# Third block's head outputs by token rows, and a router with early logits and roots by token, in a two-layer hybrid decoder step

## The reference

```python
def _mixer_c(h, hg_s, lower_bound, w_in, hg_gn, w_out):        # 8 heads of 128
    qp, fp, ip, gp = split(h @ w_in)
    f = lower_bound + (1 - lower_bound) * sigmoid(fp)
    q, k, v = silu(qp), 1 - f, ip
    o, s_new = _hgrn2(q, k, log(f), v, hg_s)                   # gated linear recurrence with carried state
    o = o * rsqrt(mean(o**2, over a head's 128) + EPS) * hg_gn * silu(gp)
    return o @ w_out, s_new

def _moe(h, w_router, b_router, wg, wu, wd):                   # h = rmsnorm(x)
    logits = h @ w_router + b_router
    top_val, top_idx = top_k(logits, 2)
    gates = scatter(softmax(top_val), top_idx)
    return sum over e of gates[:, e] * swiglu(h, wg[e], wu[e], wd[e])
```

## Time and profile before

| | |
|---|---|
| runs | 1507.21, 1500.73, 1492.23 us |
| the profiled execution: its time | 1492.97 us |
| its span | 1491.1 us |
| mean granted clock of TensorE | 0.996 |
| third block with its output projection, from its first tile to the router | about 481 to 704 us |
| router, up to the first expert product | 704.5 to 726.4 us |
| one expert round | 93.47 us |
| HBM over the span | 270 GB/s; in the rounds 382 GB/s |

### The profile page before, as it was taken

How to read it: one execution, slowest core, us unless ns; L and a number is a source line. 1 busy time by engine, 2 the same in 40 slices (tenths; PEclk the granted TensorE clock), 3 DMA queues, 4 the chain that set the end, 5 groups by cost and what they waited for, 6 DMA issues and landing times.

```text
span 1491.1 us, 22842 instructions
## 1 busy us (share of the span) xinstructions
PE 1468.7 (98%) x8429; PEld 1303.5 (87%) x8429; DVE 1123.0 (75%) x1228; ACT 912.2 (61%) x953; POOL 86.4 (6%) x96
## 2 busy tenths in 40 slices
PE   9999999999999999999999999999999999999997
PEld 8899899999999999998888888888888888888885
DVE  5766688455456577456798888988889898898987
ACT  5434655433333553343777878778787787877875
POOL 1024110000000001210200000000000000000011
PEclk9999999999999999999999999999999999999999
DMA  9477725996446443442999999999999999999994
GB/s 253 129 129 143 152 89 142 303 302 186 134 141 184 150 140 103 138 141 66 414 383 393 388 361 396 374 388 390 359 394 377 386 392 359 393 378 385 398 333 171
DMA packets 213586, 404.02 MB, mean 271 GB/s; under 512 B 13471, under 2 KB 130491, under 8 KB 213390
## 3 DMA queue, kind: packets, MB, share of 16 engines
q1 hardware_dynamic: 202976, 372.82, 71.9%
q0 software_dynamic: 6320, 22.20, 5.0%
q10 hardware_dynamic: 4222, 8.06, 1.4%
HBM read 372.75 MB, written 30.28 MB: 270 GB/s over the span
## 4 chain that ended last, share of the span: by engine, by line
PE 92%; DVE 5%; ACT 1%; issue 1%; POOL 0%; ACTq 0%; DVEq 0%; POOLq 0%
PE bank L525 27%; PE bank L527 27%; PE bank L526 27%; PE bank L754 2%; PE bank L1190 1%; PE bank L1014 1%; DVE dense_lo L1924 1%; PE bank L799 1%; PE bank L699 1%; DVE arena L2074 1%; PE bank L746 1%; PE bank L1127 1%; PE bank L675 0%; PE bank L1117 0%; PE bank L707 0%
## 5 line engine op out<-in xcount | busy, mean ns | idle before, releaser
L2414 DVE TENSOR_TENSOR w_lo<-arena,w_hi 128x2048 fp32r<-128x2048 f32 (+1 forms) x280 | 597.0, 2166 | 82.9 <-ACT w_hi L1761 82.0
L1761 ACT ACTIVATE w_hi<-arena 128x2048 fp32r<-128x2048 f32 (+1 forms) x280 | 502.1, 1820 | 117.4 <-PE bank L527 111.8
L525 PE MATMUL bank<-w_hi,xg_hi 128*128 128x512 f32 x704 | 275.6, 391 | 0.7 <-DVE w_lo L2414 0.5
L527 PE MATMUL bank<-w_hi,xg_lo 128*128 128x512 f32 x704 | 274.1, 389 | 0.0
L526 PE MATMUL bank<-w_lo,xg_hi 128*128 128x512 f32 x704 | 274.0, 389 | 0.0
L1924 DVE TENSOR_TENSOR dense_lo<-ring,dense_hi 128x2048 fp32r<-128x2048 f32 (+1 forms) x77 | 165.5, 2149 | 120.6 <-ACT dense_hi L1415 120.5
L1415 ACT ACTIVATE dense_hi<-ring 128x2048 fp32r<-128x2048 f32 (+1 forms) x78 | 140.5, 1802 | 133.1 <-PE bank L527 113.0
L525 PEld LDWEIGHTS bank<-w_hi,xg_hi 128*128 128x128 f32 x704 | 132.2, 188 | 31.0 <-issue 3.1
L527 PEld LDWEIGHTS bank<-w_hi,xg_lo 128*128 128x128 f32 x704 | 132.1, 188 | 27.7
L526 PEld LDWEIGHTS bank<-w_lo,xg_hi 128*128 128x128 f32 x704 | 132.2, 188 | 26.9
L525 PE MATMUL bank<-h_hi,dense_hi 128*128 128x320 f32 x448 | 141.9, 317 | 1.4 <-DVE h_lo_a L1994 1.1
(11 more groups left out here) (448 smaller groups left out, 2312.7 us busy)
## 6 DMA issues: line engine op xcount, KB each, us to landing
arena<-in_w_moe_down SPq DMA_DIRECT2D x176, 512.0 KB, 6.7
arena<-in_w_moe_gate SPq DMA_DIRECT2D x128, 512.0 KB, 7.3
arena<-in_w_moe_up SPq DMA_DIRECT2D x128, 512.0 KB, 7.4
arena<-in_w_moe_gate SPq DMA_DIRECT2D x64, 384.0 KB, 4.2
arena<-in_w_moe_up SPq DMA_DIRECT2D x64, 384.0 KB, 5.3
ring<-in_w_in_ab SPq DMA_DIRECT2D x32, 512.0 KB, 8.6
ring<-in_w_in_c SPq DMA_DIRECT2D x32, 512.0 KB, 4.8
expert_rows<-ZERO SPq DMA_DIRECT2D x12, 1024.0 KB, 7.8
```

The costliest lines, as they stand in the source:

```text
L525: mm(out, left[0], right[0], start=start, stop=False)
L527: return mm(out, left[1], right[0], start=False, stop=stop)
L1761: fn(WH[SLOT_OF[p]][:, 0:unit_size(p)], STAGE[:, s, 0:unit_size(p)], ACT.Copy).then_inc(S("unit_hi"), 1)
L2414: v.tensor_tensor(WL[w][:, 0:n], STAGE[:, s, 0:n], WH[w][:, 0:n].bitcast(F32), ALU.subtract).then_inc(S("unit_split"), 1)
```

## The change

Output rows. `out` puts the probabilities (128x128) and, per sample, a matrix of queries on the stationary side, and the values or the states (128 columns) on the moving side, so that the result has tokens on the partitions. The query matrix of sample s is 128x64, zero but for that sample's 8 columns: a buffer `QB` for two heads, zeroed once by POOL at the first turn, its diagonal blocks copied by ScalarE (`spread_queries`). ScalarE copies the rows to `ROWS_OF` and squares them with its accumulator, which gives the sums per token (`SSH`). Root and reciprocal are of 128x18 and 128x6 numbers; VectorE scales the rows; three transposes per head (`rows_back`) bring them back, and VectorE's gate reads the transposed bank. `sq` and `varc` go; `gate` comes behind `mixc`, and the second `rootc` stands ahead of the last head's `state`.

Router. Logits of tiles 0 to 5 are multiplied ahead of the last output tile, 6 and 7 behind it. Mean squares are taken with the tokens on the partitions, as three columns; root and reciprocal are of 128x3 numbers; logits are scaled and biased after the transposes. The rank products are fp32r instead of float32. The first weight unit's low part comes after the ranks. The first block's loops are exchanged.

```diff
-    v1 ub0 mb0 lb0 v2 wh ub1 mb1 lb1 wl turn0 v3 ub2 mb2 lb2 out0 v4 sq0 ub3 mb3 lb3 state0 turn1 v5 wh ub4 mb4 lb4 wl out1 v6 sq1 ub5 mb5 lb5 state1 turn2 v7 ub6 lb6
-    out2 v8 wh sq2 ub7 lb7 state2 turn3 wl v9 lb8 kend1 part1 out3 v10 sq3 state3 v11 wh turn4 wl g0 out4 g1 wh sq4 wl state4
-    turn5 g2 out5 g3 wh sq5 wl state5 silug0 varc0 rootc0 turn6 g4 gate0 gate1 out6 g5 wh sq6 wl gate2 gate3 state6
-    turn7 mixc0 mixc1 g6 mixc2 mixc3 out7 h0 h1 g7 h2 h3 sq7 silug1 silug2 gate4 gate5 state7 gate6 gate7 wh mixc4 mixc5 wl
-    h4 h5 varc1 rootc1 mixc6 mixc7 h6 h7
+    v1 ub0 mb0 lb0 v2 wh ub1 mb1 lb1 wl turn0 v3 ub2 mb2 lb2 out0 v4 ub3 mb3 lb3 state0 turn1 v5 wh ub4 mb4 lb4 wl out1 v6 ub5 mb5 lb5 state1 turn2 v7 ub6 lb6
+    out2 v8 wh ub7 lb7 state2 turn3 wl v9 lb8 kend1 part1 out3 v10 state3 v11 wh turn4 wl g0 out4 g1 wh wl state4
+    turn5 g2 out5 g3 wh wl state5 silug0 rootc0 turn6 g4 out6 g5 wh wl state6 turn7 mixc0 gate0 mixc1 gate1 g6 mixc2
+    gate2 mixc3 gate3 out7 h0 h1 g7 h2 h3 silug1 silug2 rootc1 state7 mixc4 gate4 mixc5 gate5 wh wl h4 h5 mixc6 gate6
+    mixc7 gate7 h6 h7
...
+        ROWS_OF = [PH[:, u, 0:3 * P].rearrange("p (i n) -> p i n", n=P) for u in range(HG)]
+        QB = region(6400, 2, NB, SMP)
...
-                    mm(b[:, 0:NT], C("inv_d"), SQF[tag][:, 0, :], start=True, stop=False)
                     pe.wait_ge(S("n3_squares"), KD)
-                    ins = mm(b[:, 0:NT], C("inv_d"), SQF[tag][:, KD - 1, :], start=False, stop=True)
+                    for i, (t0, tn) in enumerate(BLK):
+                        mm(b[0:tn, i:i + 1], SQF[tag][:, 0, t0:t0 + tn], C("inv_d")[:, 0:1], start=True,
+                           stop=False).then_inc(S("unit_used"), 1)
+                        ins = mm(b[0:tn, i:i + 1], SQF[tag][:, KD - 1, t0:t0 + tn], C("inv_d")[:, 0:1], start=False, stop=True)
+                        if i < 2:
+                            ins.then_inc(S("unit_used"), 1)
...
+            def rows_back(u):
+                pe.wait_ge(S("rows_scaled"), u + 1)
+                kind = "dve" if u in HEADS[0] else "act"
+                b = open_bank(kind)
+                for i, (t0, tn) in enumerate(BLK):
+                    ins = nc.tensor.transpose(b[:, t0:t0 + tn], ROWS_OF[u][0:tn, i, :], ident[0:tn, 0:tn])
+                close_bank(kind, ins, ("hn1", "scale", u))
...
+            def output_rows(u):
...
+                pe.wait_ge(S("queries_spread"), u + 1)
+                b = open_bank("act")
+                mm(b[:, 0:P], p[:, 0:P], values(0), start=True, stop=True)
+                mm(b[:, P:TP], p[:, P:TP], values(0), start=True, stop=False)
+                mm(b[:, P:TP], p[:, TP:384], values(1), start=False, stop=True)
+                mm(b[0:SMP, TP:384], p[:, 384:448], values(2), start=True, stop=False)
+                for s in range(NB):
+                    ins = mm(b[0:SMP, TP:384], QB[:, u % 2, s, :], ST[:, u % NST, s, :], start=False, stop=(s == NB - 1))
+                close_bank("act", ins, ("num", 1, u))
...
                     if kind == "oc" and n == len(HEADS[0]) - 1:
                         for u in HEADS[1]:
-                            head_scale(heads, u)
+                            rows_back(u)
...
+                    if kind == "oc" and k == KD - 1:
+                        pe.wait_ge(S("router_in"), 32)
+                        early = open_bank("dve", 1)
+                        logits(range(KD - 2), early)
                     gemm_tile(w, k % 2 * P, src, "dve", (kind, k), KD)
...
+            logits([KD - 2], b).then_inc(S("unit_used"), 1)
+            close_bank("dve", logits([KD - 1], b), "logit_rows")
+            mean_squares("n3")
+            after_empty(pe, "logit_rows")
...
-                    mm(b[0:tn, i * NE:(i + 1) * NE], ones[:, 0:tn], SELM[:, j, :], start=(j == 0), stop=False)
+                    mm(b[0:tn, i * NE:(i + 1) * NE], everyone[:, 0:tn], CHOSEN[:, j, :], start=(j == 0), stop=False)
...
+            def spread_queries(u):
+                if u == 0:
+                    act.wait_ge(S("queries_zero"), 2)
+                if u >= 2:
+                    after_fill(act, ("num", 1, u - 2))
...
+                fn(own, Q[:, u, TP:NT].rearrange("p (s t) -> p s t", t=TS), ACT.Copy).then_inc(S("queries_spread"), 1)
...
                 elif name == "out":
-                    free(fn(OH[:, u, :], take(("num", 1, u))[:, 0:NT], ACT.Copy))
-                elif name == "sq":
-                    after_empty(act, ("num", 1, u))
-                    fn(SQH["hn1"][u], OH[:, u, :], ACT.Square).then_inc(S("hn1_squares"), 1)
+                    b = take(("num", 1, u))
+                    fn(ROWS_OF[u][:, 0:2, :], b[:, 0:TP].rearrange("p (i n) -> p i n", n=P), ACT.Copy)
+                    fn(ROWS_OF[u][0:SMP, 2, :], b[0:SMP, TP:384], ACT.Copy)
+                    spent = (Q[:, u, 0:P], Q[:, u, P:TP], K[:, u, 0:P])
+                    for i, (t0, tn) in enumerate(BLK):
+                        ins = fn(spent[i][0:tn], b[0:tn, i * P:(i + 1) * P], ACT.Square, accum_out=SSH[0:tn, u, i:i + 1])
+                    free(ins)
...
             split_high(0, 0, 0)
...
+            act.wait_ge(S("n3_scale"), 1)
...
                 elif name == "rootc":
-                    head_reciprocals("hn1", u)
-                elif name == "mixc":
-                    dve.wait_ge(S("gated1"), u + 1)
-                    scaled_head(OH, "hn1", u)
+                    at = slice(HEADS[u][0], HEADS[u][-1] + 1)
+                    dve.wait_ge(S("hn1_roots"), u + 1)
+                    step(v.reciprocal(SSH[:, at, :], SSH[:, at, :]))
+                    for h in HEADS[u]:
+                        v.tensor_tensor(ROWS_OF[h], ROWS_OF[h], SSH[:, h, :].unsqueeze(2).to_broadcast([P, 3, P]),
+                                        ALU.mult).then_inc(S("rows_scaled"), 1)
...
-            split_low(1, 0)
-            dve.wait_ge(S("unit_split"), 1)
+            step(v.memset(RANK[:, :, :], 0.0))
             b = take("ranks")
...
+            split_low(1, 0)
+            tokens_low(0, 0, 2)
             split_low(2, 1)
-            tokens_low(0, 0, 2)
+            tokens_low(0, 1, 2)
             split_low(3, 2)
-            tokens_low(0, 1, 2)
...
                 if name == "turn":
+                    if u == 0:
+                        pool.wait_ge(S("level_up1"), 2)
+                        pool.wait_ge(S("queries_zero"), 1)
+                        g.memset(QB[:, :, :, :], 0.0).then_inc(S("queries_zero"), 1)
+                        pool.wait_ge(S("queries_zero"), 2)
                     if u % 2 == 0:
                         after_empty(pool, (("V", 1, u // 4), u % 4 // 2, 2))
                     spread(1, u)
```

More of the change, by code:

```diff
@@ L244, in trunk_kernel @@
         HEADS = ((0, 1, 2, 3, 4, 5), (6, 7))
-        SQH = {"hn0": [region(NT * u, NT) for u in range(KD)],
-               "hn1": [region(5120 + NT * u, NT) for u in range(KD)]}
+        SQH = {"hn0": [region(NT * u, NT) for u in range(KD)]}
         ROT = region(13824, H4, NT)
@@ L325, in trunk_kernel @@
         NS0 = small[:, 24:56]
+        SSH = small[:, 432:432 + 3 * HG].rearrange("p (h i) -> p h i", i=3)
         NRAW = small[:, 56:92].rearrange("p (h n) -> p h n", n=9)
@@ L330, in trunk_kernel @@
         LBT = small[:, 144:168].rearrange("p (a b) -> p a b", b=8)
+        brt = small[:, 424:424 + NE]
         QE = small[:, 168:296].rearrange("p (a b) -> p a b", b=SMP)
@@ L357, in trunk_kernel @@
         CM2 = region(7384, 3, 64)
-        SELM = rows[:, 1, 0:3 * NE].rearrange("p (i e) -> p i e", e=NE)
+        BEATEN = rows[:, 1, 0:3 * NE].rearrange("p (i e) -> p i e", e=NE)
+        AT_COUNT = AT_ARENA + 26880 + (CONST["level"][0] + 128) // 32 * 32
+        COUNT, CHOSEN = parts("count_tiles", AT_COUNT, 2, P), parts("chosen_of", AT_COUNT + 2 * P, 3, NE)
+        SELM = CHOSEN[:, :, :].bitcast(F32)
         RANK = rows[:, 2, 0:3 * NE].rearrange("p (i e) -> p i e", e=NE)
@@ L896, in _ @@
                 elif name == "weigh":
[L897 removed]
+                    piece_along(outputs(u, PB[:, u % 2, :], lambda: after_empty(pe, ("sc", 0, u)), QE[:, u % 2, :]))
                 elif name == "state":
@@ L921, in n_rows, with logits @@
                 close_bank("act", ins, "n_out")
+            def logits(ks, b):
+                for k in ks:
+                    pe.wait_ge(S("n3_value"), k + 1)
+                    ins = mm(b[0:NE, 0:NT], wrt[:, k, :], U_R[:, k, :], start=(k == 0), stop=(k == KD - 1))
+                return ins
             def projection_out(kind, src, heads):
@@ L1061, in _ @@
                     pe.wait_ge(S("vx1"), 1)
-                    piece_along(outputs(1, u, PH[:, u, :], lambda: pe.wait_ge(S("chunks_parted"), u // 4 + 1), Q[:, u, TP:NT]))
+                    output_rows(u)
                 elif name == "state":
@@ L1753, in _ @@
             projected_out("oc", "n3")
-            root("n3")
+            b = take(("n3", "ms"))
```

(20 more changed lines are left out.)

100 lines of the change are left out of this document (41 added, 59 removed).

## The result

The changed kernel takes 1502.17 us, the median of 13 runs between 1497.99 and 1509.28. The kernel before, run beside it on the same chip, takes 1493.03 (13 runs, 1491.78 to 1507.21). The ratio is 1.0057, 95% interval 1.0040 to 1.0074: slower by 0.57%, where -1.0 us was forecast. The range of 1488 to 1508 holds 1502.17, but for a poor reason: it was built around 1500.73, the median of three runs, and the middle of thirteen is 7.7 us lower. Read as a difference, the forecast missed by 10 us. That 1502.17 lies close to the 1502.6 of my second rival, the falling clock, is luck of the same kind: the rival's difference was +1.3 to +2.4, the measured one is +9.1.

What follows compares the result with a forecast made beforehand. TensorE, busy 98% of the span, was taken to bound the kernel. Terms 0, -2.9, -1.3, +1.0, +3.4, -2.2 and +1.0 summed to -1.0 us: 1492.0 profiled, 1499.7 on the median, range 1488 to 1508.

Steps and rivals of the forecast that it cites:

- second rival, the falling clock: TensorE's clock falls to half at the block's end, ahead of the projection: sum +1.3 to +2.4 us, chance 0.2.
- Term 7: First turn: POOL's zeroing of the spread queries delays the spread and head 0's outputs: +1.0 us, bounds 0 and +2.1.
- Term 1: Output products of eight heads: 24 records at 0.11 take 2.6 us per head, as before: 0.
- Term 2: Variances of heads 0 to 5: twelve products go, 3.36 us, against a 0.5 stall before head 6's outputs: net -2.9.
- Term 3: Heads 0 to 3: three transposes (0.24 us) replace each scale (0.56): -1.3 us.
- Term 4: End of the block, heads 4 to 7: longer waits outweigh TensorE's savings: +1.0 us, bounds -2.4 and +2.0.
- Term 5: Router: six logits ahead of the last tile delay it and the first expert weight transfer: +3.4 us.
- Term 6: Router, from the last tile's end to the first block of expert inputs: -2.2 us, bounds -3.5 and 0.

Runs made afterwards that it cites:

- filled waits: The changed kernel with unused identity products on TensorE ahead of its waits for the first spread and the projection's first bank; 1497.82 us, ratio 1.0019.
- late spread: The kernel before, with POOL also waiting for VectorE's second level and zeroing 1024 columns ahead of its first spread; 1500.6 us, ratio 1.0046.
- late logits: The changed kernel with all eight logits behind the last output tile; 1498.4 us, ratio 1.0034.
- root behind states: The changed kernel with the second root behind the last head's new states in every engine's order; 1500.76 us, ratio 1.0045.
- spread first: The changed kernel with POOL's first spread ahead of the zeroing of the query buffer; 1496.55 us, ratio 1.0011.
- root ahead: Changed kernel with POOL's first spread ahead of the zeroing, all logits behind the last output tile, second root behind the last head's outputs; 1493.62 us, ratio 0.9997.
- low parts first: As root ahead, with the weight split's high part earlier, its low part later, and the transposes of heads 6 and 7 later; 1489.12 us, ratio 0.9976.
- its repetition: The same kernel as low parts first, run once more; 1490.15 us, ratio 0.9971.

## Why the prediction was wrong

- **Term 7, the zeroing ahead of the spread** (+1.0, bounds 0 to +2.1) is the step that failed. I took from the one case in the earlier trace rows that a spread begun inside a split ends 0.9 after that split. The mechanism was right; what I ended with the split goes on over every VectorE instruction with two SBUF operands that follows without a gap. 567.66 + 2.27, then 0.47, then four in 1.68: the spread got no turn between any two of them. The wait was 3.0 instead of 1.0, beyond my upper bound, and with the half clock that came with it A was 6.0 longer. The Trainium skill ("SBUF — State Buffer", section "Who interferes with whom") has the rule of which instructions contend and says that the loser waits in full; on the waiting the trace agrees (4.95), and it shows besides that the wait doesn't end with the first of VectorE's instructions. On an instruction that only writes it says little: the zeroing took 0.96, but only its last 0.15 lay beside the split. I had counted only the one winner that I knew from the trace of before, and not the run of them in VectorE's own timeline, which stood there to be read.
- **The rival "the clock falls"** was right as a mechanism and too small in place: I put it at the end of the block alone, and with 0.2. It came at the first head's outputs as well, where my own term 7 had put a standing (2.7 us), ahead of the projection (1.2) and through the router (E 13.23 against 11.63 with the full clock up to 721, 1.6). That is 5.5 us, against 8.7 in all; the first block, which before had 5.4 us of half clock in it and now has 3.6, gives 0.8 back. I had waits of TensorE in terms 4 and 7 of my sum, each at its bare length.
- **Term 1, output products** (0) measured +0.29 a head: from TensorE's timeline of the second head, given below, 588.90 to 591.77 is 2.87, where before it was 582.19 to 584.77, 2.58. The four value products take 1.03 where three took 0.82, and the states 1.84 where they took 1.76. Some +2.3 over eight heads, 2.0 of it in B.

```profile
588.90 0.39 PE L796 MATMUL bank<-arena 128*128 128x128 f32 x2
589.12 0.39 PE L797 MATMUL bank<-arena 128*128 128x128 f32 x2
589.35 0.39 PE L798 MATMUL bank<-arena 128*128 128x128 f32 x2
589.66 0.43 PE L799 MATMUL bank<-arena 128*64 128x128 f32 x2
589.93 1.91 PE L801 MATMUL bank<-arena 128*64 128x128 f32 x16
591.77 0.38 PE L530 MATMUL bank<-dense_hi,h_hi 128*128 128x256 f32 x1
```

- **Term 2, variances** (-3.4, stall 0.5) was right: 3.37 gone, and a wait of 0.4 for ScalarE's query copy.
- **Term 3, scales to transposes** (-1.3) measured -0.5. Six transposes take 1.09 to the next product (661.53 to 662.62), and the four products of two scales before took 0.98 (656.10 to 657.08): by themselves they gain nothing. I had priced them by the three key transposes in the earlier trace rows, 0.24 to the next product; the rows' own take 0.54 for three. Nor is a record 0.08, as I read there: that is a third of the 0.24, and the last of the three is followed by the next product sooner than the others. What came of the term is in before's second pair of scales, which took 1.65 (660.71 to 662.36) with a wait of 0.25 for VectorE in it, where six transposes now take 1.09.
- **Term 4, end of the block** (+1.0) measured +2.25, of it 1.2 by the clock, so about +1.1 for the order of the work: right in size, with a wait at the place named, of 3.3 where I had 4 to 5. The second wait that I had there, 1.0 at the fifth head's low part, is 0.8 where the clock stays up (filled waits) and doesn't show behind products at half clock. The working behind the term, that the root's place costs this time, fell in two experiments.
- **Term 5, early logits** (+3.4) was right: 3.33.
- **Term 6, router's tail** (-2.2) is -2.4 in E where the clock stayed up the longest (11.63, I had 11.7), and -0.8 in the profiled execution. The part that I didn't see is that without early logits E is 13.7, and F no longer, so early logits give back 0.4 to 2.1 of the 3.3 that they cost: the whole of terms 5 and 6 is a bad trade.
- **The base.** The three runs given had their median 7.7 above the middle of thirteen; the profiled execution at 1492.97 was the better guide, and I had set it aside.

Stage by stage, forecast and measured: A +1.0 and +6.0; B -4.2 and -1.3; C +1.0 and +2.3; D +3.4 and +3.3; E and F -2.2 and -1.6.

## What to carry to other kernels

Ahead of an instruction on POOL that reads SBUF, look at what VectorE has queued for the next microseconds: such an instruction must be through ahead of the whole run, or it ends behind it, 1.3 us or 4.95 here. Price a wait of TensorE of some 3 us at 1.4 to 2.5 times its length (3.3 and 1.2 more in C; 2.97 and 4.5 more in the kernel before with the late spread), since the clock may fall with it, and put harmless products into it before anything more clever. When a wait goes and another of nearly the same length appears (3.3 to 2.2, then 2.1), the engine's order is not yet the right one: ask what stands ahead of the piece that is waited for last, here a weight split that nobody needed yet, and that itself stood 1.4 us for ScalarE.

## What the runs showed of the hardware

- A GpSimd product with SBUF operands, begun under VectorE's run of two-operand products, took 4.95 us at the first spread of the block in all five traces in which it began there (the changed kernel, late logits, root behind states, filled waits, before with a late spread), and 1.32 or 1.38 in all others, where it began ahead of them.
- Between 60 and 735 us the 14 traces have thirteen waits of TensorE of 2 us or more (2.09 to 3.27), and at each of them the clock fell, 1.0 to 4.4 us after the wait had begun. One of 1.3 us, between 133 and 140 us in every trace, was never followed by half clock.
- This holds in code that is the same in all kernels as well. At about 73 us TensorE waits 0.64 to 1.25 us in twelve profiles, without half clock; in the other two (spread first, filled waits) the same wait was 3.1 us, and half clock followed.
- A short wait leaves it open. At about 200 us all fourteen profiles have one of 0.8 us, and in four of them (after, root ahead, low parts first and its repetition) 3.4 us of half clock came, in one 6 us after its start, in the others at once; in the router of the kernel before the clock fell with no wait above 0.55 us ahead of it. So one profile of a kernel is not its clock: the same wait of 3.3 us ahead of the projection went with 6.8 us of half clock in two traces and with 3.4 in three.
